# Both feed-forwards make the up half by seven block products for eight; another order of work at the second one's two edges

## The chip, the cores and the metric

The kernel runs on one core of a Trainium2 chip. The metric is device time in microseconds (us), lower is better. Engines work in parallel and meet at semaphores: TensorE (PE, matmuls from SBUF into the eight banks of PSUM), VectorE (DVE), ScalarE (ACT), GpSimd (POOL) and SyncE (SP, which here only issues DMAs).

## The reference, cut to what matters

A two-layer encoder over 1040 tokens (16 meta tokens and 1024 real ones) with 1024 features. Layer 0 mixes by a Fourier part and attention, layer 1 by a gated scan (HGRN); each mixer is followed by the same kind of feed-forward, and both of these are what the change touches:

```python
def sq_relu_mlp(h, w1, w2):
    return jnp.square(jax.nn.relu(h @ w1)) @ w2
...
    for layer in range(DEPTH):
        ...
        h = h + sq_relu_mlp(rms_norm(h, mlp_norm_gain[layer]), mlp_w1[layer], mlp_w2[layer])
    return rms_norm(h, final_norm_gain)[:, N_META:]
```

`w1` is 1024x4096 (the up half), `w2` 4096x1024 (the down half). Layer 0's feed-forward works on all 1040 tokens, layer 1's on the 1024 real ones, since the meta rows are not part of the output.

## The kernel before

**Layout.** Features lie on the 128 partitions, tokens on the free axis: `h[:, k, :]` is feature block k of 8, a row of T = 1044 tokens (1040 and four of padding). A float32 product is made of three products in fp32r: x = xh + xl and w = wh + wl, and wh·xh, wh·xl and wl·xh are added up in PSUM. `wsp` holds the split weights of two *units*; a unit is one block of 1024 weights per partition, loaded by SP into `raw` (512 KB), split by POOL (`split`: one operation for the high part, one for the low), used by PE. ACT writes `xh`, DVE writes `xl`.

**Layer 0's feed-forward** (`mlp(0, ...)` on each engine). `up` makes four hidden blocks of 128 features, each by 8 (k) x 3 (parts) x 3 (column pieces `ALL`: 348, 348, 344) = 72 matmuls, all at line L1777; DVE applies relu and the norm's scale (`relu`, L1365), ACT squares (L829) and takes the high part `ah`, DVE the low part `al`. `down` multiplies four hidden blocks into the eight output blocks, 8 x 4 x 3 x 3 = 288 matmuls, and DVE adds them to `h` (L1342). Chunk c+1's `up` goes ahead of chunk c's `down`, in a hardware loop (`Fori`); the hidden blocks stay in SBUF. There are 32 up blocks (32 x 72 matmuls) and 8 down chunks.

**Layer 1's feed-forward** already works by the scheme that the change brings to layer 0. Four hidden blocks are made plainly (`up`), the other 28 as 14 *pairs* (`PAIRS`). In a pair, two weight blocks x two halves of the features, and two halves of the features x two halves of the tokens, form a 2x2 block product, which is made by 7 products instead of 8 (Strassen-Winograd). The token side's sums S1 to S4 are made once (`ts`, `t3s` on DVE, high parts `t1h` to `t4h` on ACT, low parts `t1l` to `t4l` on DVE); the weight side's sums `sw0`, `sw1`, `sw2` per pair on POOL (`add`, L627), their high parts on ACT (`high`, L1042), the low ones on POOL (`low`, L631) into `wop`, which has four operand places. A product (`product`, L2162) is 4 x 3 = 12 matmuls of 512 columns into one PSUM bank, of which it has eight in turn (`bank_of`); DVE combines the banks into four hidden halves (`hid`, L1685 to L1721), applies relu (L1675), ACT squares and stores them to a DRAM buffer `hidden`. The down half needs them again: `hidden_load` (SP, L573), `hidden_high` (ACT, L1077), `hidden_low` (DVE, L1679). The first down block has its own lines (L2198), the rest L1777.

**Around layer 1's feed-forward.** Eight output blocks of the scan's last two heads (12 matmuls each, tiles `oh`, `ol`) are added to `h` by DVE (L1341). For each k, DVE does: add, then (`finish`) the low part `xl` (L1180), which waits for ACT's `xh` (L703), then the norm's sum of squares (`ssq`, L1186), which waits for ACT's square. PE makes the norm sums (L1813) behind up unit 0 and the norm's broadcast (L1834) in the middle of unit 1, in banks 6 and 7; it waits there for ACT, which has sums S2 ahead of the norm's copies in its queue.

## Time and profile before

| | |
|---|---|
| median of 3 runs | 2748.2 us (2740.7 to 2748.81) |
| the profiled execution | 2747.0 us, span 2745.2 us |
| mean granted clock of TensorE | 0.986 of full speed |
| PE, PEld busy | 97%, 87% of the span |
| DVE, ACT, POOL busy | 52%, 30%, 37% |
| layer 0's feed-forward on PE | about 562 to 1309 us |
| layer 1's feed-forward on PE | about 2032 to 2723 us |

The span runs from the first to the last instruction of the profiled execution, and 1.8 us lie around it. A busy PE says that matmuls are in flight, not how densely; how many of them end per microsecond in a stretch is what tells the pace. PEld is the loading of the stationary operand (weights): each matmul has one.

### The profile page before, as it was taken

The page shows a single profiled execution, that of the slowest core. Times are in us where ns is not written, and L with a number is a line of the kernel's source. Part 1 is how long each engine was busy: PE and PEld are TensorE (multiplying, and loading weights), DVE is VectorE, ACT ScalarE, POOL GpSimd, SP SyncE. Part 2 cuts the span into 40 slices and gives each one's busy share as a digit, 9 for nine tenths or more (in the row PEclk, how much of TensorE's full clock was granted, in tenths as well). Part 3 has the DMA queues.
Part 4 walks back from the last instruction along what each step waited for, and adds up shares of the span by engine and source line. Part 5 has one row for each costly group of instructions (what it writes and reads, how often), then busy time and mean ns, then how long its engine had stood idle before and what let it go on. Part 6 is the DMA issues. An engine that isn't in the chain of part 4 may idle for free.

```text
span 2745.2 us, 43661 instructions
## 1 busy us (share of the span) xinstructions
PE 2663.8 (97%) x18291; PEld 2399.4 (87%) x18291; DVE 1422.3 (52%) x1686; ACT 835.6 (30%) x1337; POOL 1026.8 (37%) x501
## 2 busy tenths in 40 slices
PE   7998999999999999999999999999989999999998
PEld 7897998999999999999888888888868888788887
DVE  5287887442222222225567777877475444443434
ACT  3115887121100110012234444444233333210003
POOL 3230000344434443444323232323436787544441
PEclk9998999999999999999999999999989999999999
DMA  4110000111111111113111111112112323322221
GB/s 159 30 33 8 0 0 8 47 39 47 46 47 47 47 47 47 47 47 109 39 40 36 36 32 40 32 40 83 41 39 89 119 97 126 123 100 92 93 99 70
DMA packets 177072, 159.30 MB, mean 58 GB/s; under 512 B 6290, under 2 KB 158180, under 8 KB 176902
## 3 DMA queue, kind: packets, MB, share of 16 engines
q1 hardware_dynamic: 166966, 135.25, 15.7%
q10 hardware_dynamic: 9936, 21.51, 2.0%
q8 instruction: 140, 2.29, 0.3%
q14 instruction: 30, 0.25, 0.0%
HBM read 131.57 MB, written 25.17 MB: 57 GB/s over the span
## 4 chain that ended last, share of the span: by engine, by line
PE 83%; DVE 9%; issue 4%; ACT 3%; DMA 1%; POOL 0%; SPq 0%; ACTq 0%; DVEq 0%; POOLq 0%
PE ps L1777 63%; PE ps L2162 9%; PE ps L1911 3%; PE ps L2036 2%; PE ps L2004 1%; DVE kk L1467 1%; ACT prob L781 1%; PE ps L1861 1%; PE ps L2074 1%; ACT kk L879 1%; DVE kk L1464 1%; DVE ssq L1186 1%; PE ps L2198 1%; PE ps L1879 0%; DVE y L1262 0%
## 5 line engine op out<-in xcount | busy, mean ns | idle before, releaser
L604 POOL TENSOR_TENSOR wsp<-raw,ones 128x1024 fp32r<-128x1024 f32 x169 | 330.8, 1957 | 1591.8 <-PE ps L1777 1553.5
L1777 PE MATMUL ps<-xh,wsp 128*128 128x348 f32 (+2 forms) x3968 | 878.2, 347 | 14.3 <-DVE xl L1164 8.0
L1777 PEld LDWEIGHTS ps<-xh,wsp 128*128 128x128 f32 x3968 | 672.4, 190 | 62.6 <-issue 16.6
L1777 PE MATMUL ps<-xl,wsp 128*128 128x348 f32 (+2 forms) x1984 | 478.3, 342 | 0.0
L606 POOL TENSOR_TENSOR wsp<-raw,wsp 128x1024 fp32r<-128x1024 f32 x169 | 465.8, 2756 | 13.2
L1777 PEld LDWEIGHTS ps<-xl,wsp 128*128 128x128 f32 x1984 | 346.9, 190 | 24.5
L1777 PE MATMUL ps<-ah,wsp 128*128 128x348 f32 (+1 forms) x1536 | 286.7, 321 | 0.0
L1777 PE MATMUL ps<-hh,wsp 128*128 128x512 f32 x992 | 271.1, 395 | 0.0
L1777 PEld LDWEIGHTS ps<-ah,wsp 128*128 128x128 f32 x1536 | 250.9, 188 | 0.0
L1777 PEld LDWEIGHTS ps<-hh,wsp 128*128 128x128 f32 x992 | 186.3, 188 | 44.2
L1342 DVE TENSOR_TENSOR h<-h,ps 128x1044 f32<-128x1044 f32 x72 | 89.3, 1240 | 254.9 <-PE ps L1777 254.9
L1341 DVE TENSOR_TENSOR h<-h,ps 128x1024 f32<-128x1024 f32 x80 | 97.5, 1219 | 211.0 <-PE ps L1777 204.8
L829 ACT ACTIVATE tmp<-tmp 128x1044 f32<-128x1044 f32 x32 | 34.5, 1078 | 555.7 <-DVE tmp L1365 555.7
L1365 DVE SCALAR_TENSOR_TENSOR tmp<-ps,rms 128x1044 f32<-128x1044 f32 x32 | 39.9, 1246 | 271.9 <-PE ps L1777 271.9
L1777 PE MATMUL ps<-al,wsp 128*128 128x348 f32 (+1 forms) x768 | 162.7, 320 | 0.0
L1777 PE MATMUL ps<-hl,wsp 128*128 128x512 f32 x496 | 155.5, 394 | 0.0
L1777 PEld LDWEIGHTS ps<-al,wsp 128*128 128x128 f32 x768 | 129.0, 188 | 0.0
L905 ACT ACTIVATE kp<-kk 128x512 f32<-128x512 f32 x112 | 65.6, 635 | 163.0 <-PE ps L2036 145.0
L1777 PEld LDWEIGHTS ps<-hl,wsp 128*128 128x128 f32 x496 | 93.3, 188 | 22.3
L2162 PE MATMUL ps<-xh,wop 128*128 128x512 f32 x336 | 109.9, 394 | 0.0
L1077 ACT ACTIVATE hh<-tmp 128x1024 fp32r<-128x1024 f32 x32 | 34.0, 1061 | 243.2 <-DMA tmp<-hidden 189.2
L703 ACT ACTIVATE xh<-h,small 128x1044 fp32r<-128x1044 f32 x24 | 28.1, 1170 | 187.0 <-DVE h L1342 151.5
(275 smaller groups left out, 4153.5 us busy)
## 6 DMA issues: line engine op xcount, KB each, us to landing
raw<-in_w SPq DMA_DIRECT2D x128, 512.0 KB, 3.9
raw<-in_c_w_in SPq DMA_DIRECT2D x40, 512.0 KB, 3.8
tmp<-hidden SPq DMA_DIRECT2D x32, 512.0 KB, 4.2
hidden<-hid ACTq DMA_DIRECT2D x56, 256.0 KB, 2.0
raw<-in_ab_w_in SPq DMA_DIRECT2D x12, 512.0 KB, 4.0
xst<-in_x SPq DMA_DIRECT2D x8, 512.0 KB, 6.7
raw<-in_ab_w_out SPq DMA_DIRECT2D x8, 512.0 KB, 3.9
h_kept<-h ACTq DMA_DIRECT2D x8, 512.0 KB, 2.6
```

The source lines that it names most:

```text
L604: nc.gpsimd.tensor_tensor(wsp[:, slot, 0, :], raw[:, slot, :], one, ALU.mult).then_inc(w_high, 1)
L606: nc.gpsimd.tensor_tensor(wsp[:, slot, 1, :], raw[:, slot, :], wsp[:, slot, 0, :], ALU.subtract).then_inc(w_split, 1)
L829: A(tmp[:, j % 2, t0:t1], tmp[:, j % 2, t0:t1], ACT.Square).then_inc(l_s, 1)
L905: ins = A(dst, src, ACT.Copy)
L1077: A(hh[t // CH % 2][:, t % CH, real], tmp[:, t % 2, real], ACT.Copy).then_inc(l_h, 1)
L1341: return V.tensor_tensor(real_pieces(h[:, k, :]), real_pieces(h[:, k, :]), real_outp(s), ALU.add).then_inc(z_free, 1)
L1342: return V.tensor_tensor(pieces(h[:, k, :]), pieces(h[:, k, :]), outp(s), ALU.add).then_inc(z_free, 1)
L1365: V.scalar_tensor_tensor(pieces(tmp[:, j % 2, :]), outp(s), 0.0, pieces(rms[:]), ALU.max, ALU.mult).then_inc(z_free, 1)
L1777: ins = M(ps[:, 3 * s + c, 0:n], w(a, k), b(k)[:, c0:c0 + n], start=(k == first and a == 0 and b is xa), stop=(k == last and a == 1))
L1911: ins = M(ps[0:TT, c, 0:n], q[:, gg, i * TT:(i + 1) * TT], k[:, gg, c * CB:c * CB + n], start=(q is qh and k is kh), stop=(q is ql))
L2036: ins = M(ps[size * b:size * (b + 1), 6 + lv % 2, chunk * size:(chunk + 1) * size], left, right, start=True, stop=True)
L2162: ins = M(product_bank(p, s), wop[:, g % 4, side, k * P:(k + 1) * P], x(k), start=(k == 0 and side == 0 and x is high), stop=(k == CH - 1 ...
```

## The change

Layer 0's feed-forward is now made as layer 1's: one function `feed(layer)` on every engine serves both, unrolled, with no hardware loop. Layer 0's halves of the tokens are 520 wide (`HALF_T = (520, 512)`), more than a PSUM bank holds, so a product is 4 x 3 x 2 = 24 matmuls of 260 columns into two banks, and there are four such places in turn instead of eight. The hidden rows of layer 0 go to DRAM and back too. The softmax of the scan's lower bounds (small operations on DVE and an Exp on ACT) moves from ahead of layer 0's feed-forward to behind it.

In both layers S4 with weight block (1,1) is now product 2 and the block (1,0) product 3 (they were 3 and 2), so DVE's order of combining changes with them, and in the last pair the four `hidden_low` stand earlier.

At the start of layer 1's feed-forward the norm is put behind: ACT makes all eight `xh`, then the squares; DVE adds and makes `xl` for all eight k, then the sums of squares. PE makes the norm sums after the sixth k of unit 1 and the broadcast after the third k of unit 2, in banks 2 and 5; unit 2 has banks 6 and 7, unit 3 banks 0 and 1. ACT has the norm's copies ahead of S2.

```diff
+HALF_T = (TOK // 2, SEQ // 2)
...
+        def product_bank(layer, p, s):
 
-        def product_bank(p, s):
-            return ps[:, bank_of(7 * p + s), :]
+            g = 7 * p + s
+            if layer == 0:
+                b = (0, 6, 2, 4)[g % 4]
+                return ps[:, b:b + 2, 0:HALF_T[0] // 2]
+            return ps[:, (2, 5, 6, 7, 0, 1, 3, 4)[g % 8], :]
...
+                else:
+                    for k in range(KT):
+                        act.wait_ge(z_free, HG_LAST + k + 1)
+                        A(xh[:, k, :], h[:, k, :], ACT.Copy, scale=small[:, col + k:col + k + 1]).then_inc(n_hi, 1)
+                    for k in range(KT):
+                        if k >= 3:
+                            act.wait_ge(n_ssq, 7 * n + k - 9)
+                        A(ssq[:] if k == 0 else tmp[:, k % 2, :], h[:, k, :], ACT.Square).then_inc(n_sq, 1)
...
+                else:
+                    unit(u, 0, e, 0, hx, lx, x_ready(n), cols=cols)
+                    unit(u + 1, 1, e + 1, 1, hx, lx, gap=[lambda: norm_sum(n)], cuts=(6,), cols=cols)
+                    unit(u + 2, 0, e + 2, 2, hx, lx, gap=[lambda: norm_bcast(n)], cuts=(3,), cols=cols, free=e)
+                    unit(u + 3, 1, e + 3, 0, hx, lx, cols=cols, free=e + 1)
...
+                    else:
+                        p, s = divmod(g - (4, 8)[layer], 7)
+                        if s == 0:
+                            pe.wait_ge(t_cp, PAIRS * layer + p + 1)
+                        else:
+                            pe.wait_ge(t_rd, r0 + 6 * p + s)
...
+                            if layer == 0:
+                                M(out[:, 0, :], left, x(k)[:, 0:width // 2], start=start, stop=stop)
+                                ins = M(out[:, 1, :], left, x(k)[:, width // 2:width], start=start, stop=stop)
+                            else:
+                                ins = M(out, left, x(k), start=start, stop=stop)
...
+                u, e = U_DN[layer], E_DN[layer]
+                pe.wait_ge(l_l, l0 + CH)
+                pe.wait_ge(t_rd, r0 + 6 * PAIRS - (1 if layer == 0 else 4))
```

**PE, the up half of layer 0.** Before, a block of the plain up half (`xh`, `xl` the input's parts, `wsp` split weights); the same three parts repeat for each k and block.

```order
L1777 MATMUL ps<-xh,wsp 128x348 x2
L1777 MATMUL ps<-xh,wsp 128x344
L1777 MATMUL ps<-xl,wsp 128x348 x2
L1777 MATMUL ps<-xl,wsp 128x344
L1777 MATMUL ps<-xh,wsp 128x348 x2
```

Now, the first k of product 0 of pair 0 (`wop` holds the weight side's sums and blocks):

```order
L1954 MATMUL ps<-xh,wop 128x260
L1955 MATMUL ps<-xh,wop 128x260
L1954 MATMUL ps<-xl,wop 128x260
L1955 MATMUL ps<-xl,wop 128x260
```

28 blocks of 72 matmuls are replaced by 98 products of 24.

**DVE, the start of layer 1's feed-forward.** Before (L1341 adds an output block to `h`, L1180 is the low part, L1186 the sum of squares):

```order
L1341 TENSOR_TENSOR h<-h,ps 128x1024 x3
L1180 SCALAR_TENSOR_TENSOR xl<-h,small,xh 128x1044
L1341 TENSOR_TENSOR h<-h,ps 128x1024
L1180 SCALAR_TENSOR_TENSOR xl<-h,small,xh 128x1044
L1186 TENSOR_TENSOR ssq<-ssq,tmp 128x1044
L1341 TENSOR_TENSOR h<-h,ps 128x1024
```

Now:

```order
L1324 TENSOR_TENSOR h<-h,ps 128x1024 x3
L1393 SCALAR_TENSOR_TENSOR xl<-h,small,xh 128x1044
L1324 TENSOR_TENSOR h<-h,ps 128x1024
L1393 SCALAR_TENSOR_TENSOR xl<-h,small,xh 128x1044
...
L1398 TENSOR_TENSOR ssq<-ssq,tmp 128x1044 x7
L1337 SCALAR_TENSOR_TENSOR ts<-h,small,x_99 128x512 x4
```

The seven sums of squares have left the loop over k and stand behind it.

**DVE, the last pair and the first hidden rows.** Before, in layer 1 (`hl` is the low part of a reloaded hidden row):

```order
L1685 TENSOR_TENSOR uv<-p_100,ps 128x512
L1688 TENSOR_TENSOR hid_103<-p_100,ps 128x512
L1692 TENSOR_TENSOR hid_105<-uv,ps 128x512
L1679 TENSOR_TENSOR hl_115<-tmp,hh_113 128x1024
L1700 TENSOR_TENSOR uv<-uv,ps 128x512
L1679 TENSOR_TENSOR hl_115<-tmp,hh_113 128x1024
L1704 TENSOR_TENSOR hid_105<-hid_105,ps 128x512
L1707 TENSOR_TENSOR hid_106<-uv,ps 128x512
L1679 TENSOR_TENSOR hl_115<-tmp,hh_113 128x1024
L1712 TENSOR_TENSOR hid_104<-uv,ps 128x512
L1679 TENSOR_TENSOR hl_115<-tmp,hh_113 128x1024
```

Now, in layer 0 (layer 1 has the same order with 512 and 1024 columns):

```order
L1383 TENSOR_TENSOR uv_107<-p_0_106,ps 128x520
L1383 TENSOR_TENSOR hid_0_111<-uv_107,ps 128x520
L1379 TENSOR_TENSOR hl_122<-tmp,hh_120 128x1040 x2
L1383 TENSOR_TENSOR hid_0_109<-p_0_106,ps 128x520
L1383 TENSOR_TENSOR uv_107<-uv_107,ps 128x520
L1379 TENSOR_TENSOR hl_122<-tmp,hh_120 128x1040 x2
L1383 TENSOR_TENSOR hid_0_111<-hid_0_111,ps 128x520
L1383 TENSOR_TENSOR hid_0_112<-uv_107,ps 128x520
L1383 TENSOR_TENSOR hid_0_110<-uv_107,ps 128x520
```

All four low parts stand ahead of the two operations that read product 5; before, the fourth stood behind everything.

## Rows read from the trace of the kernel before

**Rows 1.** The page, part 1: busy time and share of each engine.

```profile
PE 2663.8 (97%) x18291; PEld 2399.4 (87%) x18291; DVE 1422.3 (52%) x1686; ACT 835.6 (30%) x1337; POOL 1026.8 (37%) x501
```

**Rows 2.** The page, part 4: the chain that ended last, by engine.

```profile
PE 83%; DVE 9%; issue 4%; ACT 3%; DMA 1%; POOL 0%; SPq 0%; ACTq 0%; DVEq 0%; POOLq 0%
```

**Rows 3.** Stretches: length, busy (count) of PE, PEld, DVE, ACT, POOL; PEclk, DMA share, GB/s.

```profile
795.00:977.00 182.00, 181.99 (x1148) 181.99 (x1149) 46.91 (x32) 17.26 (x16) 73.98 (x32) 1.00 0.16 47
979.00:1309.00 330.00, 330.00 (x2084) 330.00 (x2083) 105.28 (x72) 44.26 (x41) 134.41 (x58) 1.00 0.19 60
2087.40:2338.00 250.60, 250.60 (x1081) 202.77 (x1080) 111.43 (x139) 93.26 (x154) 200.48 (x142) 1.00 0.33 110
2378.00:2723.00 345.00, 345.00 (x1485) 278.74 (x1484) 145.01 (x99) 46.17 (x45) 150.12 (x60) 1.00 0.24 86
...
1996.17:2031.57 35.40, 26.82 (x98) 19.81 (x96) 26.10 (x19) 14.11 (x15) 9.42 (x4) 0.86 0.10 31
2031.57:2087.31 55.74, 51.91 (x217) 41.03 (x218) 41.36 (x42) 21.09 (x31) 22.24 (x10) 0.94 0.17 57
...
2363.91:2377.71 13.80, 13.80 (x49) 11.07 (x50) 2.57 (x2) 1.06 (x1) 4.27 (x2) 0.81 0.42 152
```

**Rows 4.** The chain in order of time: start, us, what; a run of 128-column matmuls.

```profile
1434.69 5.13 PE ps L2004 x46
```

**Rows 5.** PE and PEld groups by form: busy us, mean ns of one, idle before.

```profile
L1777 PEld LDWEIGHTS ps<-ah,wsp 128*128 128x128 f32 x1536 | 250.9, 188 | 0.0
L2004 PEld LDWEIGHTS ps<-vt,aa 128*128 128x128 f32 x128 | 19.9, 191 | 1.9 <-DVE st L1430 1.2
L2049 PE MATMUL ps<-ident,kk 128*128 128x128 f32 x112 | 14.8, 272 | 0.0
```

**Rows 6.** DVE in order of time, start of layer 1's feed-forward, and one combination.

```profile
2002.85 1.22 DVE L1341 TENSOR_TENSOR h<-h,ps 128x1024 f32<-128x1024 f32 x1
2005.30 1.31 DVE L1180 SCALAR_TENSOR_TENSOR xl<-h,small,xh 128x1044 fp32r<-128x1044 f32 x1 [1.24 <-ACT xh L703]
2006.52 1.24 DVE L1186 TENSOR_TENSOR ssq<-ssq,tmp 128x1044 f32<-128x1044 f32 x1
2010.13 2.42 DVE L1180 SCALAR_TENSOR_TENSOR xl<-h,small,xh 128x1044 fp32r<-128x1044 f32 x1 [1.24 <-ACT xh L703]
2012.47 3.38 DVE L1186 TENSOR_TENSOR ssq<-ssq,tmp 128x1044 f32<-128x1044 f32 x1
...
2224.80 0.68 DVE L1721 TENSOR_TENSOR hid<-uv,ps 128x512 f32<-128x512 f32 x1
```

**Rows 7.** PE in order of time, the same start: its three largest waits there.

```profile
2017.04 1.22 PE L1777 MATMUL ps<-oh,wsp 128*128 128x512 f32 x2 [5.01 <-DVE h L1341]
...
2042.38 0.70 PE L1777 MATMUL ps<-xh,wsp 128*128 128x512 f32 x2 [0.84 <-DVE xl L1180]
...
2055.78 1.53 PE L1834 MATMUL ps<-tmp,ones 116*128 116x348 f32 x2 [2.99 <-ACT rms L718]
```

**Rows 8.** All engines in order of time: last pair of products to the first down block.

```profile
2354.93 1.06 ACT L1077 ACTIVATE hh<-tmp 128x1024 fp32r<-128x1024 f32 x1 [4.15 <-DMA tmp<-hidden]
...
2360.58 1.06 ACT L1077 ACTIVATE hh<-tmp 128x1024 fp32r<-128x1024 f32 x1 [2.39 <-DMA tmp<-hidden]
...
2361.67 2.19 DVE L1679 TENSOR_TENSOR hl<-tmp,hh 128x1024 fp32r<-128x1024 f32 x1 [0.50 <-ACT hh L1077]
...
2363.91 1.22 PE L2198 MATMUL ps<-hh,wsp 128*128 128x512 f32 x2 [3.70 <-DVE hl L1679]
```

**Rows 9.** All engines in order of time: an Exp's table load; the scan's first stores.

```profile
583.42 1.28 ACT L824 ACT_TABLE_LOAD   x1
...
1319.82 1.23 DVE L1409 TENSOR_TENSOR zf<-ps,rms 128x1044 f32<-128x1044 f32 x1 [4.77 <-issue]
...
1324.88 1.23 DVE L1413 TENSOR_TENSOR zf<-ps,rms 128x1024 f32<-128x1024 f32 x1 [3.83 <-PE ps L1777]
```

More of the change, by code:

```diff
@@ L496, in _, with pair_load @@
-            mlp(0, U_MLP0)
+                for j in range(CH):
+                    load(U_UP[layer] + j, j % 2, k8, v1[:, :, j * P:(j + 1) * P])
+                def pair_load(p, part, free, count):
+                    c0 = CH * P + 2 * P * p
+                    sp.wait_ge(free, count)
+                    nc.sync.sem_inc(c_sp, 1)
+                    nc.sync.dma_start(k4(raw[:, part, :]), v1[:, CH * part:CH * (part + 1), c0:c0 + 2 * P]).then_inc(t_land[part], 16)
+                pair_load(0, 0, w_split, U_DN[layer] - 1)
@@ new lines, in feed, with down_load @@
+                pair_load(0, 1, w_split, U_DN[layer])
+                for p in range(1, PAIRS):
+                    pair_load(p, 0, t_add, 4 * (PAIRS * layer + p))
+                    pair_load(p, 1, t_low, PRODUCTS * layer + 7 * p - 3)
+                def down_load(i):
+                    c, j = i // CH, i % CH
+                    if i == 0:
+                        sp.wait_ge(t_add, 4 * PAIRS * (layer + 1))
+                    if i == 1:
+                        sp.wait_ge(t_low, PRODUCTS * (layer + 1) - 3)
+                    load(U_DN[layer] + i, i % 2, k4, v2[:, c, :, j * 2 * P:(j + 1) * 2 * P])
@@ new lines, in hidden_load @@
+                def hidden_load(t):
+                    if t < 2:
+                        sp.wait_ge(s_first[t], 32 * (layer + 1))
+                    else:
+                        sp.wait_ge(l_l, 32 * layer + t - 1)
+                    if t >= CH:
+                        for half in range(2):
+                            sp.wait_ge(s_hid[2 * (t % 2) + half], 16 * (PAIRS * layer + t // 2 - 1))
+                    nc.sync.sem_inc(c_sp, 1)
+                    nc.sync.dma_start(tmp[:, t % 2, span(layer, 0, 2)], hidden_rows[t][:, 0:2 * HALF_T[layer]]).then_inc(s_re[t % 2], 16)
@@ L498, in _ @@
+                hidden_load(0)
+                down_load(0)
+                down_load(1)
+                hidden_load(1)
+                for t in range(2, CH):
+                    hidden_load(t)
+                for i in range(2, 32):
+                    down_load(i)
+                    if i + 2 < 32:
+                        hidden_load(i + 2)
+            feed(0)
             v_c = c_w_in.rearrange("(k p) (s n) -> p k s n", p=P, s=5)
@@ L612, in _ @@
+            feed(0)
+            with pool.Fori((U_DN[0] + 2) // 2, (U_HG + 40) // 2) as i:
                 for slot in range(2):
@@ L823, in _ @@
+            feed(0)
+            norm(2)
             act.wait_ge(g_lb, 3)
             A(lbt[:, :, :], lbt[:, :, :], ACT.Exp).then_inc(g_lba, 1)
[L826 to L847 removed]
@@ L1122, in _ @@
-            keep(PAIRS - 1, 3, 1)
-            for t in range(2 * CH, 32):
-                act.wait_ge(z_ready, E_DN + 8 * (t // CH - 1))
-                hidden_high(t)
-            for k in range(KT):
-                finish(4, k, False)
+            feed(1)
             act.wait_ge(n_sum, 4)
@@ L1348, in _ @@
+            feed(0)
+            norm(2)
             stat2 = qsc[:].rearrange("p a b -> p (a b)")[:, 0:16]
@@ L1725, in _ @@
[L1725 to L1735 removed]
+            feed(1)
@@ L1955, in _ @@
                      m_ready if j == 0 else None)
-            def up(u, e, c0, cols, ready=None, n=None):
-                for j in range(CH):
-                    unit(u + j, j % 2, e + j, j % 2, hx, lx, ready if j == 0 else None,
-                         gap=[lambda: norm_bcast(n)] if (n and j == 1) else None, cols=cols)
-                    if n and j == 0:
-                        norm_sum(n)
             def down(u, e, l, high, low, cols):
@@ L1991, in o_products @@
+            feed(0)
             def o_products(hd):
@@ L2203, in _ @@
[L2203 to L2210 removed]
+            feed(1)
```

920 lines of the change are left out of this document (407 added, 513 removed).

## The prediction, made before the changed kernel was run

> **What bounds the kernel now.** I read the page's shares first: PE is busy for 97% of the span, no other engine for more than 52% [rows 1], and the chain that ended last is PE for 83% and "issue" for 4% [rows 2]. So what counts is how fast matmuls pass, and where PE waits. A busy share does not tell the pace, so next come the stretches with their counts [rows 3]. In layer 0's feed-forward 2084 matmuls take 330.0 us, 158.4 ns each (1148 in 182.0 give 158.5), for 348, 348 or 344 columns, 346.7 in the mean. In layer 1's products 1081 take 250.6 us, 231.8 ns, and in its down half 1485 take 345.0 us, 232.3 ns, for 512 columns. PE has no idle time in any of these, and POOL, the busiest other engine, is at 200.5 of 250.6 us in the products. Layer 0's feed-forward is thus bound by the pace of PE and by nothing else. PE waits in two places that the change touches: at the start of layer 1's feed-forward [rows 3, 7] and between its products and its down half [rows 8].
>
> **Layer 0's up half, the large term.** Removed: 28 blocks x 72 = 2016 matmuls x 158.4 ns = 319.3 us. Added: 14 pairs x 7 products x 24 = 2352 matmuls of 260 columns. In columns this is an eighth less (seven for eight), but it is a sixth more matmuls, each with its own weight load. No row has fp32r matmuls of 260 columns. Two rows at the full clock give a line: (232.3 - 158.4) / (512 - 346.7) = 0.447 ns per column and 3.4 ns fixed, so 260 columns take 119.6 ns, if the moving side sets the pace. The weight side must be able to follow: 46 matmuls of 128 columns, each with a load of 128x128, pass in 5.13 us, one per 111.5 ns [rows 4]. That is the nearest row for a load's floor, and it is below 119.6. So I take 119.6 ns: 2352 x 0.1196 = 281.3 us, a gain of 38.0 us. The ends are 111.5 ns (262.2 us, a gain of 57) and the 132 ns of 112 transposes in 14.8 us [rows 5] (310.5 us, a gain of 9). The first row is nearer than the second in what it does (accumulating matmuls, not transposes), but the line passes through matmuls of this very form, and I take the line.
>
> A rule that speaks against the change: layer 0's stretches show PEld busy for all of their 330.0 us, the 512-column stretches for 278.7 of 345.0 [rows 3]. The Trainium skill, Perfetto Trace Analysis, section "Identifying the Most-Contended Engine", says to judge TensorE's headroom by the share of time in which weight loads are busy; by that there is none left here, and more loads cost in full. This is the second rival below. Against it stands that a load lasts 188 ns at a pace of one per 158.4 ns, and 191 ns at a pace of one per 111.5 ns [rows 3 to 5]: loads overlap, so a full PEld row is no full loader. The same skill, TensorE: Matmul & The Clock Gate, section "LDWEIGHTS (loading the stationary operand)", gives columns / 1.2 ns, an estimate of 107 ns for 128; the 111.5 ns agree with it.
>
> What else must keep up in a pair of 168 x 0.1196 = 20.1 us: POOL has 200.5 us per 250.6 of the products stretch, that is 15.6 us per pair of 19.5 [rows 3], and the same operations here; ACT and DVE have 7.3 and 8.7. PSUM gives each product four places in turn instead of eight, so a bank must be read within three products, 8.6 us, of being filled. The latest read in a pair is the last combination: DVE starts it at 2224.80, 1.0 us behind its product's end after a doubled relu [rows 6]. Cost 0, with room. Sums, loads and hidden rows of layer 0's start lie beside units 1 to 3 (34 us of PE; DVE has 32 sums and low parts of about 0.68 us and four relus of 1.2, 27 us); cost 0, and up to 3 us if DVE's relus come late.
>
> **Layer 0's hidden rows by DRAM, a new wait.** Before, PE went from up to down without a gap. Layer 1 shows what the new way costs: PE waits 3.70 us for the fourth hidden low part [rows 8], and the next 48 matmuls take 13.80 us at a mean clock of 0.81 where they would take 48 x 0.2323 = 11.2 [rows 3], 2.6 us more after the pause. The chain behind the wait is not DVE's order: hidden row 1 lands at 2354.93 behind two weight loads, only its low part frees the buffer for row 3, which lands by 2360.58, is copied in 1.06 and subtracted in 2.19 [rows 8]. In layer 0 PE also needs product 5 read, by two combinations of 0.68 us [rows 6] that stand behind the fourth low part: 3.7 + 1.4 = 5.1 us, less 0.4 since its last four products are 0.1 us longer each, plus 2.6 for the clock: **a loss of 7.3 us**. Ends: 2 (the pause closed) and 12.
>
> **Layer 1's transition.** Low parts 0 and 1 move ahead of a combination. Low part 0 comes about 1.7 us earlier, low part 1 does not, since it waits for its DMA [rows 8], and the fourth hangs on that one. 0 us, ends -2 and +1.
>
> **Layer 1's start.** Per k, DVE is in a ring with ACT: it starts the add to h at 2002.85, waits 1.24 us for ACT's xh, starts the low part at 2005.30 and the square sum of 1.24 us at 2006.52, 4.9 us in all [rows 6], while PE has 12 x 0.2323 = 2.8 us of work per k. Without the square sum it is 3.7 us. The first add can start when PE's first block from 1996.17 is done, at 1999.0 or just behind; eight k of 3.68 us end at about 2028.6; a POOL split beside it stretches two operations from 1.31 and 1.24 to 2.42 and 3.38 us [rows 6], 3.3 us, and a second one perhaps 2: some 2034, against 2042.4 now [rows 7]. PE's last output block waits for add 5, about 2022, ends at 2024.8, and unit 0 follows: 8 x 6 x 0.2323 = 11.2 us, ending at 2036 with its last k just met. Then three units of 11.2 us, 1.7 for the norm sums, 2.0 for the broadcast and about 1 for what is left of ACT's copy (now 2.99 [rows 7], since S2 is no longer ahead of it): 2036 + 38.3 = 2074 to 2077, taken as 2075.8. The products start at 2087.3 now [rows 3]: **a gain of 11.5 us**. The seven square sums, late by now, take 8.6 us from about 2034 and are due at 2036 + 8.4 = 2044.4; that is tight and may cost 1 to 3 us, as may the diagonal behind them. By another way: PE's work from 1996.17 to 2087.31 is 288 matmuls x 0.2323 + 3.7 = 70.6 of 91.1 us, so 20.5 us are lost to waits and the low clock (0.86 and 0.94 [rows 3]), and a little more than half comes back. Ends: 5 and 16.
>
> **The scan's start.** The bounds' small operations, with a table load of 1.28 us on ACT [rows 9], now come ahead of the scan's first store at 1319.82, about 2.4 us with the waits. The second store waits for PE until 1324.88, after 3.83 us of idling [rows 9], and covers it. 0 us; without that cover 2.4.
>
> **The sum.** The profiled execution took 2747.0 us. 2747.0 - 38.0 + 7.3 + 0 - 11.5 + 0 = 2704.8. The median of the runs is 1.2 us above it: **2706 us**.
>
> **Rivals.**
> 1. *The weight side and the moving side get in each other's way.* At 260 columns a load's floor of 111.5 ns is only 8 ns under the matmul, and no row shows fp32r matmuls so near to it. At 132 ns the up half takes 310.5 instead of 281.3 us: 2735. For it speaks that both fp32r paces lie a tenth above one column per cycle at 2.4 GHz (144.4 and 213.3 ns); against, that the line's fixed part is small.
> 2. *Slower: loads cannot pass faster than one per 158.4 ns*, as the full PEld row suggests. Then 2352 x 0.1584 = 372.6 us, 53.3 more than before, and 2747.0 + 53.3 - 4.2 + 1.2 = 2797. It decides from 137.5 ns on, where 2352 matmuls take 323.5 us, the old 319.3 and the 4.2 of the two edges. Against it: 111.5 ns [rows 4].
> 3. *The floor itself*: the matmuls of 260 columns go at 111.5 ns, 262.2 us, 2687. For it, that a smaller share of columns may take the tenth with it; against, the line.
> 4. *The edges do not give what they should*: DVE's square sums hold PE at the norm sums, or the new ring is stretched by more splits, a gain of 5 instead of 11.5, and layer 0's transition costs 12 instead of 7.3: 2717.
>
> **How the numbers follow.** Forecast (pace 116 to 125 ns, edges as worked out) 0.62, with a range of its own of 2694 to 2722; rival 1 0.13; rival 2, with all from 137.5 ns up, 0.07; rival 3 0.08; rival 4 0.08; nothing of this but a time near the old one, 0.02. A measurement of this kernel tells 0.3%, 8 us, from no change. Faster by over 0.3%: 0.90; within: 0.03; slower: 0.07. The range from 2686 to 2735 takes in rivals 1, 3 and 4 and leaves out rival 2.
>
> **What would show it.** The count of matmuls in a stretch inside layer 0's products: 20 us should hold 167 (126 in rival 2, 152 in rival 1), with no idle time of PE. PE's first down block of layer 0 should show an idle of 4 to 6 us, released by DVE's combination or low part, and about 20 matmuls at the low clock. In layer 1's start the low parts should end near 2034 on the old scale, with the products starting 11 to 12 us sooner after the last scan block; the square sums stand in a row behind them. The transition in layer 1 should still show some 3.7 us. The forecast is wrong if the pace at 260 columns leaves the line, or if DVE's lag in a pair reaches three products so that PE idles on the combinations.

## The result, and the profile after

The changed kernel takes **2695.94 us** (median of 4 runs, 2693.65 to 2697.76); the kernel before, run beside it on the same chip, 2746.26 us (2740.7 to 2748.81). The ratio is 0.9828, 95% interval 0.9812 to 0.9844. Forecast was 2706, with a range from 2686 to 2735. The profiled execution took 2697.76 us, span 2696.0, at a mean granted clock of 0.989. The kernel before had a span of 2745.2, so 49.2 us have to be accounted for.

The page of the kernel after, part 1 (answers to [rows 1]) and the first line of part 4 (answers to [rows 2]):

```profile
PE 2617.3 (97%) x18627; PEld 2355.3 (87%) x18627; DVE 1551.0 (58%) x1844; ACT 913.7 (34%) x1496; POOL 1124.3 (42%) x599
...
PE 82%; DVE 9%; issue 4%; ACT 3%; DMA 1%; POOL 1%; SPq 0%; ACTq 0%; DVEq 0%; POOLq 0%
```

PE's shares hardly move (97% again, 82% of the chain for 83%); it has 336 matmuls more and is busy for 46.5 us less. So the gain shows in the pace and in the waits, not in the shares. These are stretches of the kernel after, with the columns of [rows 3]: layer 0's products, layer 0's down half, layer 1's products, layer 1's down half.

```profile
635.00:865.00 230.00, 230.00 (x1918) 230.00 (x1917) 117.45 (x124) 81.01 (x137) 176.05 (x127) 1.00 0.32 110
920.00:1260.00 340.00, 340.00 (x2152) 340.00 (x2152) 144.75 (x100) 43.86 (x43) 150.97 (x60) 1.00 0.28 99
2041.34:2300.00 258.66, 258.66 (x1117) 209.52 (x1118) 119.07 (x144) 96.02 (x162) 212.25 (x149) 1.00 0.33 113
2378.00:2515.00 137.00, 137.00 (x591) 110.66 (x590) 55.26 (x37) 12.73 (x12) 61.91 (x24) 1.00 0.27 97
```

230.00 / 1918 is 119.9 ns for each matmul of 260 columns. PEld is full there as it was at 158.4 ns [rows 3], and POOL, DVE and ACT are at 77%, 51% and 35%: PE is still the only bound.

Now the two places where PE waited before, in the kernel after. First the PE rows with the largest waits (and the norm's sums and broadcast, L1748 and L1769) from the scan's last output blocks (`oh`) to product 1 of layer 1 (`t2h`); they answer to [rows 7]:

```profile
1975.99 0.73 PE L1712 MATMUL ps<-oh,wsp 128*128 128x512 f32 x2 [1.72 <-DVE h L1324]
...
1987.06 0.70 PE L1712 MATMUL ps<-xh,wsp 128*128 128x512 f32 x2 [0.67 <-issue]
...
2007.91 1.99 PE L1748 MATMUL ps<-ones,ssq 128*116 128x1 f32 x18 [1.18 <-DVE ssq L1398]
...
2016.80 2.15 PE L1769 MATMUL ps<-tmp,ones 116*128 116x348 f32 x6
...
2041.34 0.47 PE L1957 MATMUL ps<-t2h,wop 128*128 128x512 f32 x1 [1.53 <-issue]
```

The first block of `oh` starts at 1959.60, so product 1 comes 81.74 us behind it. Before, the same two points were 1996.17 and 2089.93, 93.76 us apart. I use this distance below, since it takes in the waits on both sides of product 0. The waits of 5.01, 0.84 and 2.99 us [rows 7] have become 1.72, none and none, and two new ones of 1.18 and 1.53 have come. [Rows 7] calls its three the largest, which they are not: the kernel before also waits 1.48 us at 2008.99 and 1.77 at 2026.69, where the kernel after has 0.32 and 0.62.

Then the first down block in layer 0, where there was no wait before, and in layer 1 (answers to the last row of [rows 8]):

```profile
896.70 0.71 PE L1993 MATMUL ps<-hh,wsp 128*128 128x348 f32 x3 [1.92 <-issue]
...
2314.91 0.73 PE L1993 MATMUL ps<-hh,wsp 128*128 128x512 f32 x2 [3.69 <-DVE hl L1379]
```

| place | us against before | how it is read |
|---|---|---|
| kernel's start to the first mixing block | +0.9 | 474.70 to 475.60, nothing of the edit |
| layer 0, up half | -37.3 | 2016 x 0.1584 = 319.3; now 2352 x 0.1199 = 282.0 |
| layer 0, up to down | +2.1 | idle 1.92; the next 72 matmuls take 11.61 |
| layer 0, hardware loop gone | -3.1 | two idle pieces of 0.97 and 0.76, and 158.1 instead of about 158.5 ns in the rest |
| the scan's start | +0.8 | same waits; the low clock behind the wait of 3.73 us lasts longer |
| layer 1's start | -12.0 | 93.76 to 81.74; 2.9 of it is low clock that the same code does not always have (run 2) |
| layer 1, up to down | -0.9 | same wait; the 48 matmuls behind it 12.91 for 13.80, again as in run 2 |
| rest | +0.3 | 49.2 less the sum of the rows above |

The scan's start, in the kernel before and then in the kernel after, 7.00 us from where PE goes on behind its wait of 3.73 us:

```profile
1343.98:1350.98 7.00, 7.00 (x119) 6.75 (x123) 1.64 (x3) 0.00 (x0) 0.00 (x0) 0.76 0.01 2
```

```profile
1306.62:1313.62 7.00, 7.00 (x89) 6.94 (x90) 1.63 (x3) 0.00 (x0) 0.00 (x0) 0.60 0.00 1
```

From the norm's sums to this point both kernels take 34.25 us (1309.73 to 1343.98, 1272.37 to 1306.62), so the small operations that moved here cost nothing. All traces of kernels with the change show the longer low clock, and none of the three without it does; why isn't shown.

### The profile page after: what moved, and what is told of

Read it like the earlier page. It is cut to its first block, busy times and chain, and to the rows that moved or that the text cites. A ratio compares the mean times of both kernels' runs of the same rounds, so it can differ in the third digit from the quotient of the medians.

```text
span 2696.0 us, 44722 instructions
## 1 busy us (share of the span) xinstructions
PE 2617.3 (97%) x18627; PEld 2355.3 (87%) x18627; DVE 1551.0 (58%) x1844; ACT 913.7 (34%) x1496; POOL 1124.3 (42%) x599
## 4 chain that ended last, share of the span: by engine, by line
PE 82%; DVE 9%; issue 4%; ACT 3%; DMA 1%; POOL 1%; SPq 0%; ACTq 0%; DVEq 0%; POOLq 0%
PE ps L1712 52%; PE ps L1957 9%; PE ps L1954 5%; PE ps L1955 5%; PE ps L1846 3%; PE ps L2055 2%; PE ps L2023 1%; PE ps L1993 1%; DVE kk L1551 1%; DMA tmp<-hidden 1%; ACT prob L782 1%; PE ps L1796 1%; PE ps L2093 1%; ACT kk L995 1%; DVE kk L1548 1%
## 5 line engine op out<-in xcount | busy, mean ns | idle before, releaser
L1712 PE MATMUL ps<-xh,wsp 128*128 128x348 f32 (+2 forms) x2624 | 625.2, 359 | 11.4 <-DVE xl L1147 7.3
L1712 PE MATMUL ps<-hh,wsp 128*128 128x348 f32 (+1 forms) x2480 | 546.2, 350 | 0.0
L1712 PEld LDWEIGHTS ps<-xh,wsp 128*128 128x128 f32 x2624 | 451.8, 190 | 57.6 <-issue 11.5
L1712 PEld LDWEIGHTS ps<-hh,wsp 128*128 128x128 f32 x2480 | 428.8, 188 | 44.1
L1712 PE MATMUL ps<-xl,wsp 128*128 128x348 f32 (+2 forms) x1312 | 335.4, 353 | 0.0
L1712 PE MATMUL ps<-hl,wsp 128*128 128x348 f32 (+2 forms) x1240 | 313.9, 350 | 0.0
L1712 PEld LDWEIGHTS ps<-hl,wsp 128*128 128x128 f32 x1240 | 218.1, 188 | 22.3
L616 POOL TENSOR_TENSOR wop<-sw,wop 128x512 fp32r<-128x512 f32 x112 | 144.3, 1298 | 69.5 <-ACT wop L853 69.4
L616 POOL TENSOR_TENSOR wop<-raw,wop 128x512 fp32r<-128x512 f32 x84 | 132.4, 1576 | 67.9 <-ACT wop L853 67.9
L1373 DVE SCALAR_TENSOR_TENSOR hid<-hid,rms 128x520 f32<-128x520 f32 (+1 forms) x112 | 150.4, 1361 | 0.9
```

What stands on the lines that cost most here:

```text
L616: nc.gpsimd.tensor_tensor(operand(g, 1), a, operand(g, 0), ALU.subtract).then_inc(t_low, 1)
L1373: V.scalar_tensor_tensor(hid_[b][:], hid_[b][:], 0.0, rms[:, span(layer, b % 2)], ALU.max, ALU.mult).then_inc(t_relu, 1)
L1712: ins = M(ps[:, 3 * s + c, 0:n], w(a, k), b(k)[:, c0:c0 + n], start=(k == first and a == 0 and b is xa), stop=(k == last and a == 1))
```

## The experiments

Each was timed beside the kernel before on the same chip; the medians of the kernel before were 2742.75 to 2744.01 us there, 2 to 3.5 us below the 2746.26 above. Edits are to the kernel after unless it is said otherwise. All ratios are to the kernel before.

**1. The pace of a matmul with its load, by itself.** A kernel that leaves out the encoder and runs series of matmuls, each with a load of 128x128 and nothing to wait for:

```diff
+            for n, count in SERIES:
+                for i in range(count):
+                    bank, k = i // 8 % 8, i % 8
+                    ins = nc.tensor.matmul(ps[:, bank, 0:n], wr[:, k, :], xr[:, 0:n], start=(k == 0), stop=(k == 7))
```

> Leaves out the whole encoder: PE runs fp32r matmuls of one width after another, 128x128 weights, a weight load for each, eight accumulating in a PSUM bank (512, 348, 260, 240, 224, 208, 176, 128, 64, then 260 and 512 again). It measures the pace of the disputed width by itself. Theory of the line (0.447 ns per column and 3.4 ns fixed, until the load's floor of about 111 ns takes over): 232 ns at 512, 159 at 348, 120 at 260, 111 at 240, and from 224 columns down a floor near 107 to 112 ns that no longer falls with the width. Theory that load and matmul get in each other's way near the floor (rival 1 of the prediction): the pace leaves the line above 240 columns, 125 to 132 ns at 260. Theory of the full PEld row (rival 2): no pace under 158 ns at any width.

This kernel took 284.88 us in its one run. PE by form (busy us, mean ns of one with its latency; the 260 and 512 columns are two series each, in part at the low clock), then stretches inside the first series of 512 and of 260 columns, and the series of 240, 128 and 64:

```profile
L102 PE MATMUL ps<-xr,wr 128*128 128x260 f32 x384 | 47.9, 288 | 0.0
...
L102 PE MATMUL ps<-xr,wr 128*128 128x64 f32 x192 | 39.1, 388 | 0.0
L102 PE MATMUL ps<-xr,wr 128*128 128x240 f32 x192 | 21.7, 275 | 0.0
L102 PE MATMUL ps<-xr,wr 128*128 128x208 f32 x192 | 21.6, 275 | 0.0
...
L102 PE MATMUL ps<-xr,wr 128*128 128x128 f32 x192 | 21.6, 275 | 0.0
L102 PE MATMUL ps<-xr,wr 128*128 128x348 f32 x96 | 15.4, 321 | 0.0
```

```profile
22.00:38.00 16.00, 16.00 (x72) 13.27 (x71) 0.00 (x0) 0.00 (x0) 0.00 (x0) 1.00 0.00 1
...
56.00:74.00 18.00, 18.00 (x154) 18.00 (x153) 0.00 (x0) 0.00 (x0) 0.00 (x0) 1.00 0.00 1
79.00:96.00 17.00, 17.00 (x154) 17.00 (x153) 0.00 (x0) 0.00 (x0) 0.00 (x0) 1.00 0.00 1
166.00:182.00 16.00, 16.00 (x146) 16.00 (x145) 0.00 (x0) 0.00 (x0) 0.00 (x0) 1.00 0.00 1
187.00:221.00 34.00, 34.00 (x161) 34.00 (x161) 0.00 (x0) 0.00 (x0) 0.00 (x0) 0.50 0.00 0
```

From 240 columns down to 128 the series take the same 21.6 or 21.7 us for 192, some 112 ns each. That is a floor that no longer falls with the width, and it is where the 111.5 ns of [rows 4] had put it. At 260 columns a stretch of 18.00 us holds 154 matmuls with the two or three that lie across its ends, 118 to 119 ns for each whole one, on the line (119.6) and above the floor; 348 columns take 158 to 160 ns (15.4 us for 96, the last one's latency included). The floor ends between 240 and 260 columns: halves of 260 lie just outside, so an eighth fewer columns is nearly an eighth less time. At 512 columns 16.00 us hold 72 matmuls, one or two of them across the ends, 227 ns each, where the encoder has 232.3: a line through this run's own two paces would give about 121 ns for 260 columns, 2 to 3 ns above what it measures. So the line's fit to within 1 ns in the encoder is in part luck; that 260 columns lie above the floor is not. Loads do not slow the matmuls of 260 columns down (rival 1) and do not pass at one per 158 ns only (rival 2).

**2. The hardware loop of the kernel before, unrolled on PE.**

```diff
-                with pe.Fori(0, 3) as i:
+                for i in range(3):
```

> The kernel before with the hardware loop of layer 0's feed-forward written out on PE alone (the same matmuls in the same order, the loops of the other engines kept). Theory: the loop costs PE about 3 us, 1.7 us of idle time at its two ends (0.96 and 0.77 us between the pieces of the chain) and 0.3% of the pace inside; without it 2743 us, ratio 0.999, no idle time of PE at 794 and 978 us and 157.9 to 158.1 ns per matmul in the loop's stretch. Rival: the 3 us of layer 0 that the terms of the prediction do not cover came from something else in the changed kernel (other order of up and down, hidden rows by DRAM); then no change here, 2746.

Measured: 2742.33 us (2739.32 to 2743.94, 10 runs) against 2744.01, ratio 0.9999 (0.9987 to 1.001). The kernel before has two idle pieces at the loop's passes, the unrolled one has none: the chain shows one piece from the norm to the end of the feed-forward. PE rows of before, then that piece of the unrolled kernel (start, us, what):

```profile
795.01 0.75 PE L1777 MATMUL ps<-xh,wsp 128*128 128x348 f32 x3 [0.97 <-issue]
...
978.66 0.74 PE L1777 MATMUL ps<-xh,wsp 128*128 128x348 f32 x3 [0.76 <-issue]
```

```profile
584.90 724.74 PE ps L1777 x4572
```

The 1.7 us of idling are the loop's. The pace is 724.74 / 4572 = 158.5 ns with the loop gone, so the 158.1 ns of the kernel after is not the loop's doing. It shows in the down half alone (the plain up units of the kernel after take 28.52 us for 180, 158.4 ns); what it is stays open. 1.7 us are 0.06%, too little for the medians.

In layer 1 this kernel has the code of the kernel before, and its trace shows how far two executions of the same code differ there. Its start of layer 1's feed-forward (1995.84 to 2031.23 to 2083.94; [rows 3] has the same two stretches of the kernel before) and the 12.91 us behind its layer 1 transition:

```profile
1995.84:2031.23 35.39, 24.84 (x98) 18.57 (x96) 26.10 (x19) 14.10 (x15) 9.42 (x4) 0.95 0.11 30
2031.23:2083.94 52.71, 48.90 (x217) 38.88 (x218) 42.24 (x42) 20.86 (x31) 22.23 (x10) 1.00 0.16 55
2360.69:2373.60 12.91, 12.91 (x49) 10.34 (x50) 2.46 (x2) 1.06 (x1) 4.28 (x2) 0.87 0.45 162
```

The large waits are there as in the kernel before (5.01 and 2.99 us), but the clock behind the 2.99 us stayed at 1.00, and from the first output block to product 1 are 90.87 us (1995.84 to 2086.71), not 93.76. Behind the transition 49 matmuls pass in 12.91 us as in the kernel after; the kernel before took 13.80. So 2.9 and 0.9 of the 49.2 us are low clock of its profiled execution, and no doing of the change.

**3. Layer 1's start, both parts undone**: the old ring (each k finished with its square sum) and the norm's old place and banks. ACT's order is still that of the new function, with the norm's copies ahead of the sums S2.

```diff
-                        A(xh[:, k, :], h[:, k, :], ACT.Copy, scale=small[:, col + k:col + k + 1]).then_inc(n_hi, 1)
...
+                for k in range(KT):
+                    finish(n, k)
...
-                    unit(u + 1, 1, e + 1, 1, hx, lx, gap=[lambda: norm_sum(n)], cuts=(6,), cols=cols)
-                    unit(u + 2, 0, e + 2, 2, hx, lx, gap=[lambda: norm_bcast(n)], cuts=(3,), cols=cols, free=e)
+                    norm_sum(n)
+                    unit(u + 1, 1, e + 1, 1, hx, lx, gap=[lambda: norm_bcast(n)], cols=cols)
+                    unit(u + 2, 0, e + 2, 0, hx, lx, cols=cols)
```

> The changed kernel with both edits at the start of layer 1's feed-forward undone: square sums back in the ring over k on ACT and DVE, norm sums behind unit 0 and broadcast in unit 1, banks as before. Theory: all of the 12.3 us there come from these two edits: 2696 + 12 = 2708, ratio to before 0.986, last low part about 43 us behind the first add, three large waits of PE (5, 1 and under 3 us). Rival: part of the gain is from ACT's new order of the norm's copies, which stays: 2705 to 2706.

Measured: 2700.97 us (2700.76 to 2703.46), ratio 0.9855 (0.9835 to 0.9874). From the first output block (1958.50) to product 1 (2046.36) are 87.86 us, not 93.8: 5.9 of the 12.0 us were still there, more than either expectation had.

**4. Layer 1's start, the ring alone undone**, the norm at its new place (the first part of the diff above).

> The changed kernel with only the ring undone (ACT and DVE do high part, low part, square and square sum for each k in turn); PE's norm sums in unit 1 and broadcast in unit 2 stay. Theory: the ring is worth the 8 to 9 us by which unit 0 now starts and ends earlier, the place of the norm the rest (no wait for DVE's diagonal and ACT's copy in the middle of unit 1): 2696 + 8 to 9 = 2704 to 2705. Rival: the place of the norm alone is worth nothing, and this is as slow as with both undone, 2708.

Measured: 2703.26 us (2699.9 to 2703.6), ratio 0.9856 (0.9836 to 0.9876); 1958.96 to 2047.18, 88.22 us.

**5. The new ring with the norm at its old place** (the second part of the diff above).

> The new kernel with its new ring (low parts first, square sums behind) but with the norm at its old place in layer 1: norm sums behind unit 0, broadcast in the middle of unit 1, banks 6 and 7. Theory (the two halves of the new start belong together): the seven square sums end 48.3 us after the first output block of the scan's last head (2007.91 against 1959.60 in the new kernel), unit 0 ends some 39.5 us after it, so PE waits 8 to 9 us at the norm sums and runs 2 us at the low clock behind them; the two waits of 1.18 and 1.53 us go. From the first output block to product 1: 81.7 + 8.5 + 2 - 2.7 = 89.5 us, within 88 to 92, and the time is 2704 us. Rival (the new place of the norm is worth nothing by itself, as it is with the old ring, where it gave -0.4 us): 82 us and 2696 us.

Measured: 2701.61 us (2698.6 to 2702.78), ratio 0.9846 (0.9831 to 0.9861); 1959.71 to 2047.99, 88.28 us. PE in order of time, waits at the norm's sums and then the broadcast:

```profile
2004.49 3.64 PE L1748 MATMUL ps<-ones,ssq 128*116 128x1 f32 x18 [5.98 <-DVE ssq L1398]
...
2015.41 2.15 PE L1769 MATMUL ps<-tmp,ones 116*128 116x348 f32 x6
```

The wait was 5.98 us, not 8 to 9, as the square sums were quicker here: 9.35 us for seven, with no POOL split beside them, against 12.88 in the kernel after. The 18 small matmuls then took 3.64 us instead of 1.99, at a low clock.

**6. In the kernel before, ACT's norm copies ahead of S2**, and nothing else:

```diff
             norm_root(3)
+            norm_copy(3)
             sum_high(4, t2h[:, 0, :], ts[:, 0, :])
             sum_high(5, t2h[:, 1, :], ts[:, 1, :])
-            norm_copy(3)
```

> The kernel before with one edit: in layer 1 ACT makes the norm's copies ahead of the two sums of S2 (they were behind them). With both the ring and the norm's place as before, the new kernel's layer 1 start was 5.9 us shorter than that of the kernel before, and this order of ACT is what I hold for the cause. Theory: PE's wait of 2.99 us at the broadcast and the low clock behind it (about 2.9 us) go; from the first output block to product 1 of layer 1 88 us for 93.8, and 2738 us for 2744, ratio 0.998. Rival (something else of the new function does it, such as the copies of h for x12 that stand behind all eight k there, or the swapped products): the wait at the broadcast goes or shrinks, but another takes its place within 10 us, 92 to 94 us, ratio 1.000.

Measured: 2740.34 us (2735.11 to 2742.22, 11 runs) against 2742.75, ratio 0.9988 (0.9978 to 0.9997). 1991.08 to 2078.95 are 87.87 us. The broadcast is one piece without a wait, where [rows 7] had 2.99 us:

```profile
2046.25 2.25 PE L1834 MATMUL ps<-tmp,ones 116*128 116x348 f32 x6
```

Stretches of this kernel and of the kernel before, 49.70 us from the first `xh` matmul of layer 1's feed-forward on (columns as in [rows 3]):

```profile
2026.47:2076.17 49.70, 48.86 (x216) 38.88 (x217) 41.76 (x42) 20.51 (x31) 21.05 (x10) 1.00 0.16 54
```

```profile
2031.57:2081.27 49.70, 45.87 (x191) 36.12 (x192) 41.36 (x42) 19.53 (x30) 20.93 (x9) 0.93 0.16 54
```

The same time holds 216 matmuls at a clock of 1.00, or 191 at 0.93 with a wait: 25 matmuls x 0.2323 = 5.8 us. But not all of that is the edit. The kernel of run 2 has the old order and the wait of 2.99 us, and 90.87 us for this distance, with no low clock behind the wait. Against it the edit brings 3.0 us, which is the wait itself; the other 2.9 us are low clock that one execution of the old code had and another had not. The medians differ by 2.4 us, and the interval of the ratio reaches from about 1 to 6 us, so it holds both. This one reordering made 3.0 us of the gain at layer 1's start, and 5.9 only against the one profiled execution. The traces so far make a table, us from the first output block to product 1, each number one execution:

| | norm's old place | norm's new place |
|---|---|---|
| old ring, ACT copies behind S2 | 93.76 (before); 90.87 (run 2) | not run |
| old ring, ACT copies first | 87.86; 87.87 in the kernel before | 88.22 |
| new ring, ACT copies first | 88.28 | 81.74 (after); 81.73 (runs 8 and 10); 83.79 (run 7) |

The ring and the norm's place are worth nothing one by one and 4 to 6.5 us together; the ratios say the same, 0.9846 to 0.9856 without one or both against 0.9828, 5 to 8 us, though the intervals touch. With the old ring PE waits for the last `xl`, wherever the norm is; with the new ring and the old place it waits for the square sums.

**7. Hidden row 1 loaded ahead of the two weight loads**, in both layers:

```diff
                 hidden_load(0)
+                hidden_load(1)
                 down_load(0)
                 down_load(1)
-                hidden_load(1)
```

> The changed kernel with hidden row 1 loaded ahead of the first two weight loads of the down half, in both layers (SP's order alone). Theory: the pause between products and down half hangs on row 1 that lands behind two weight loads of 512 KB; with row 1 there early, low part 1, row 3 and low part 3 come 3 to 5 us sooner, and PE waits under 0.5 us in layer 1 (now 3.70 and 1.7 to 2.6 us of low clock behind it) and 0.5 in layer 0 (now 1.9): 2696 - 6 = 2690. Rival: DVE's order or the reload of rows 2 and 3 itself sets the pause, and it stays within 1 us: 2695 to 2696.

Measured: 2689.25 us (2686.01 to 2692.4), ratio 0.9797 (0.9781 to 0.9814). PE at the two transitions, then the stretch behind layer 1's, in this kernel:

```profile
893.67 0.71 PE L1993 MATMUL ps<-hh,wsp 128*128 128x348 f32 x3 [1.58 <-issue]
...
2310.96 0.72 PE L1993 MATMUL ps<-hh,wsp 128*128 128x512 f32 x2 [0.54 <-DVE hl L1379]
```

```profile
2310.96:2323.87 12.91, 12.91 (x55) 10.47 (x56) 5.54 (x7) 1.06 (x1) 7.63 (x4) 1.00 0.46 162
```

and the same length in the kernel after:

```profile
2314.91:2327.82 12.91, 12.90 (x49) 10.41 (x50) 4.19 (x5) 1.06 (x1) 4.27 (x2) 0.87 0.46 162
```

In layer 1 the wait fell from 3.69 to 0.54 us, and the clock stayed at 1.00: 6 matmuls more in 12.91 us, 1.4 us. The chain that the prediction named behind this wait (row 1's DMA behind the weight loads, and row 3 behind row 1) is the right one. In layer 0 the wait moved from 1.92 to 1.58 only: there something else was last, and the trace has DVE's second combination that reads product 5 end at 893.57, 0.1 us before PE goes on.

At the norm's sums in layer 1, which the edit does not touch, this execution lost 3.2 us to the clock: the same 48 matmuls, from the sums to the broadcast, in this kernel and then in the kernel after, both behind a wait of 1.18 us:

```profile
2005.07:2017.13 12.06, 12.06 (x48) 10.15 (x49) 9.02 (x14) 3.35 (x7) 3.56 (x2) 0.72 0.01 2
```

```profile
2007.91:2016.80 8.89, 8.88 (x48) 7.57 (x49) 8.86 (x12) 3.37 (x7) 3.56 (x2) 1.00 0.01 2
```

**8. The four hidden low parts at their old places.**

```diff
-                    if final:
-                        hidden_low(0)
-                        hidden_low(1)
                     dve.wait_ge(t_done, g0 + 7 * p + 4)
...
+                    if final:
+                        hidden_low(3)
```

> The changed kernel with the four low parts of the last pair at their old places among DVE's combinations (one behind products 3, 4, 5 and 6 each). Theory of the prediction: the new places bring layer 1 nothing, its pause stays at 3.7 us, since low part 1 waits for its row; layer 0's pause changes by less than 1.5 us: 2695 to 2697. Rival: the earlier places are why layer 0's pause is 1.9 and not 5 us; with the old ones it is 4 to 5 us, with 2 us of low clock behind it: 2700.

Measured: 2698.64 us (2698.38 to 2698.99), ratio 0.9835 (0.9819 to 0.9852). Layer 1's wait is 3.70 us for 3.69: the order there is worth nothing, as forecast. In layer 0 it is worth something, 3.64 us for 1.92, where the theory had allowed less than 1.5 us and the rival had said 4 to 5. The fourth low part and POOL's split are beside each other (DVE, POOL, PE):

```profile
895.01 2.79 DVE L1379 TENSOR_TENSOR hl<-tmp,hh 128x1040 fp32r<-128x1040 f32 x1
...
894.36 2.35 POOL L651 TENSOR_TENSOR wsp<-raw,wsp 128x1024 fp32r<-128x1024 f32 x1 [0.98 <-PE ps L1957]
...
897.85 0.76 PE L1995 MATMUL ps<-hh,wsp 128*128 128x348 f32 x3 [3.64 <-DVE hl L1379]
```

and the clock is low behind the longer wait, in this kernel and then in the kernel after:

```profile
897.85:909.46 11.61, 11.61 (x63) 11.61 (x64) 2.49 (x2) 1.07 (x1) 4.28 (x2) 0.85 0.51 182
```

```profile
896.70:908.31 11.61, 11.61 (x73) 11.61 (x74) 2.90 (x3) 1.07 (x1) 5.17 (x3) 1.00 0.52 182
```

**9. Run 7, and the weight sums of pair 0 ahead of its first low part on POOL**, to take away the wait of 1.53 us at product 1:

```diff
                     landed(p, 0)
-                    low(g, weight(0, 0))
+                    if p:
+                        low(g, weight(0, 0))
...
+                    if p == 0:
+                        low(g, weight(0, 0))
```

> Row 1 loaded early as in the run before, and POOL makes the sums sw1 and sw0 of pair 0 ahead of its first low part, in both layers, while it idles. Theory: the wait of 1.53 us ahead of product 1 of layer 1 (high part of sw0 at 2038.99, low part until 2041.2) goes too: 2688, 1.5 us under the run with the early row. Rival: that wait comes from ACT, whose first high part stands behind S4's four, and it stays.

Measured: 2688.31 us (2685.38 to 2694.43), ratio 0.9794 (0.9776 to 0.9813). The wait is gone, but this execution, like that of run 7, had the low clock at the norm: 18 small matmuls of 2.99 us instead of 1.99 behind the same wait of 1.18, and from their start (2007.65) to the broadcast (2019.74) 12.09 us against 8.89. 1959.34 to 2042.57 are 83.23 us, against 83.79 in run 7, whose wait at product 1 was only 0.41 us. Whether the edit is worth its 1.5 us isn't settled: the medians of runs 7 and 9 are 1 us apart.

**10. Run 7, and in layer 0 the two combinations that read product 5 ahead of the fourth low part.**

```diff
                         hidden_low(2)
-                        hidden_low(3)
+                        if layer == 1:
+                            hidden_low(3)
...
                     combine(p, 5, hid_[3], uv_, ALU.add).then_inc(t_rd, 1)
+                    if final and layer == 0:
+                        hidden_low(3)
```

> The new kernel with hidden row 1 loaded ahead of the two weight loads in both layers (as in sp_early) and, in layer 0 alone, DVE's two combinations that read product 5 ahead of the fourth hidden low part. In sp_early PE still waits 1.58 us at layer 0's transition, and DVE starts those two combinations only at 892.28 and 892.89, behind a low part of 1.45 us from 890.91, though product 5 ends about 2.9 us before product 6's end at 892.1. Theory (the wait is for these two readers): they run by 890.9, PE waits for the fourth low part alone, which ends near 892.4: 0.3 to 0.8 us for 1.58; layer 1's transition stays at 0.5 us; total about 1 us less than sp_early, 2688, which the medians cannot tell apart. Rival (the wait is for ACT's and the DMA's row 3 and thus for the low part anyway, or DVE's low part is stretched by POOL's split): 1.5 us or more, no change.

Measured: 2686.8 us (2682.92 to 2694.95), ratio 0.9791 (0.9775 to 0.9808). Layer 0's wait became 3.64 us. The theory (0.3 to 0.8) failed; the rival's mechanism (row 3 and its low part, stretched by POOL's split) is what the trace shows, but it made the wait longer, where the rival had said no change. DVE's readers and fourth low part, then POOL's split, ACT's high part and PE:

```profile
892.60 0.69 DVE L1383 TENSOR_TENSOR hid<-hid,ps 128x520 f32<-128x520 f32 x1
893.21 0.69 DVE L1383 TENSOR_TENSOR hid<-uv,ps 128x520 f32<-128x520 f32 x1
895.51 3.43 DVE L1379 TENSOR_TENSOR hl<-tmp,hh 128x1040 fp32r<-128x1040 f32 x1 [1.62 <-ACT hh L887]
...
895.51 2.34 POOL L651 TENSOR_TENSOR wsp<-raw,wsp 128x1024 fp32r<-128x1024 f32 x1 [0.98 <-PE ps L1958]
...
894.41 1.07 ACT L887 ACTIVATE hh<-tmp 128x1040 fp32r<-128x1040 f32 x1 [3.00 <-DMA tmp<-hidden]
...
899.00 1.10 PE L1996 MATMUL ps<-hh,wsp 128*128 128x348 f32 x3 [3.64 <-DVE hl L1379]
```

The readers did run early. But row 3 came late: ACT's copies of rows 2 and 3 start 4.08 us apart here and 2.66 in run 7 (887.14 and 889.80). So the fourth low part began in the same moment as POOL's split and took 3.43 us where run 7 had 1.45. The order of issue is not why: row 3 was issued 1.15 us behind row 2 in both kernels (888.28 and 887.13 here, 885.02 and 883.87 in run 7), but took 6.10 us to land instead of 4.76. What made the DMA slower isn't shown; one execution can't tell. The median is the lowest of all, but its runs and those of runs 7 and 9 overlap, so no order among the three is claimed. Each stands some 0.3% below the changed kernel (0.9791 to 0.9797 against 0.9828).

## Why the prediction was right, and where it was not

- **Right as a whole**: forecast case, 10 us too high.
- **Layer 0's up half**: -38.0 forecast, -37.3 measured. The line through the two paces gave 119.6 ns; the kernel has 119.9, and run 1 118 to 119 in isolation. Rivals 1 (132 ns) and 2 (158.4 ns) fell by that, and rival 3 (111.5 ns) too: the floor exists, but below 260 columns. That the line hit to within 1 ns is in part luck, as run 1's own 512 columns are faster than the encoder's. That PE never idles on the combinations was right as well.
- **Layer 0's transition: mis-sized, +7.3 forecast, +2.1 measured.** The steps that failed are the two borrowed from layer 1. The wait of 5.1 - 0.4 us took layer 1's stretched low part of 2.19 us [rows 8] and its late row 1. In layer 0 the fourth low part took 1.24 us, as POOL's split began only 0.5 us before its end (894.93 against 895.39), and row 1 landed 7.5 us ahead of the products' end (887.35 against 894.8), where layer 1 before had 5.3. The two readers of product 5 behind it ended at 896.6, and PE went on at 896.70. And the 2.6 us of low clock did not come: behind 1.92 us of idling the clock stayed at 1.00, behind 3.64 (run 8) it was 0.85. The 2.6 were high even for layer 1, where run 2's kernel has 0.9 less behind the same wait. Run 8 gives what the forecast would have met without the new order of low parts: 3.64, and 10 matmuls x 0.158 = 1.6 us of low clock, 5.2 in all. So I had judged that order only in layer 1, where it is worth nothing, and not in layer 0, where it is worth 3 us between these two executions.
- **Layer 1's start**: -11.5 forecast, -12.0 measured, by other shares than the text gave and with luck. 2.9 of the 12.0 us are low clock of the one execution that both the forecast and this comparison start from; against run 2's kernel, with the old code there, the gain is 9.1 us. The ring was 3.68 us per k as forecast, two k were stretched, and the low parts ended 34.8 us behind the first output block (forecast 37.8, 2034 on the old scale). The first product's own start came 13.7 us sooner (90.98 to 77.27), and a wait at product 1 that I had not foreseen (ACT copies pair 0's first weight block only at 2033.47, behind the sums S3 and S4 in its queue; POOL's low part of it, two weight sums, ACT's high part of the second operand at 2038.99 and POOL's low part of 1.47 us from 2039.76 hang on that) took 1.5 back. The text mentioned ACT's order for "about 1" us of remaining wait; runs 3 and 6 show that this order, which I had put inside one sum, makes 5.9 of the 12.0 us, or 3.0 of the 9.1.
- **The square sums**: said to be tight, with 1 to 3 us at stake; the wait was 1.18 us.
- **Layer 1's transition**: 0 forecast. The wait is 3.69 as before; 0.9 us came from a shorter stretch at low clock, which run 2's kernel has with the old code too. Run 8 confirms the order's zero, run 7 the cause behind the wait.
- **The scan's start**: 0 forecast, +0.8 measured. The operations that moved there cost nothing, as forecast; the 0.8 is the longer low clock behind the same wait.
- **Not in the sum at all: the hardware loop.** The change removes it, and I costed that at nothing. It is 1.7 us of idling (run 2), and 1.4 us of pace that no run explains.
- The sum came to 2704.8 us for the profiled execution, which took 2697.76: 7.0 too much. Layer 0's transition makes 5.2 of it, the loop 3.1, layer 1's transition 0.9 and layer 1's start 0.5; the up half (-0.7), the scan (-0.8), the kernel's start (-0.9) and the rest (-0.3) go the other way. All of this is against the one profiled execution of the kernel before; some 3.8 us of what it measures are that execution's low clock, and without them layer 1's start would count as short of its forecast.

## What to carry to other kernels

Where two paces at full clock and a row for the load's floor are in the trace, the line and the floor together priced this change of a matmul's width to within 1 ns in the kernel, and would have missed by 2 to 3 ns with the paces of run 1; ask on which side of the floor the new width lies before anything is rearranged. A wait with several conditions must be priced at its own place: the same four DMAs, copies and low parts cost 3.7 us in one layer and 1.9 in the other, by when the rows land and whether a POOL split falls beside a DVE operation. What the low clock adds behind a wait differs from one execution to the next, so compare two executions of the same code before a difference of 3 us is put down to an edit. When two edits guard the same deadline, test them alone and together: here each alone was worth nothing.
